# A mixture-of-experts layer on one core: the smallest of experts 2 to 31 is computed last, for 64 places instead of 96

## The reference, cut to what matters

```python
def moe_ffn(h, router_w, router_b, w_up, b_up, w_down, b_down):
    tok = h.reshape(-1, d)                                   # 512 tokens
    logits = (tok @ router_w + router_b).astype(jnp.float32) # 32 experts
    top_vals, top_idx = lax.top_k(logits, TOP_K)             # 4 experts for each token
    gate_w = jax.nn.softmax(top_vals, axis=-1)
    ...
    gu = lax.ragged_dot(x_sorted, w_up, group_sizes) + b_up[e_sorted]    # 1024 -> 2048
    g, u = gu[:, :D_EXPERT], gu[:, D_EXPERT:]
    g = jnp.minimum(g, SWIGLU_LIMIT)
    u = jnp.clip(u, -SWIGLU_LIMIT, SWIGLU_LIMIT)
    act = (u + 1.0) * (g * jax.nn.sigmoid(SWIGLU_ALPHA * g))
    out = lax.ragged_dot(act, w_down, group_sizes) + b_down[e_sorted]    # 1024 -> 1024
    out = out * gate_w.reshape(-1)[order][:, None].astype(out.dtype)
    y = jax.ops.segment_sum(out, token_of, num_segments=n_tok)
```

## Time and profile before

| | us |
|---|---|
| median of three runs | 1942.35 |
| the profiled execution, its own time | 1940.7 |
| its span, first to last instruction | 1938.9 |
| PE busy in it | 1831.4 (94%) |
| mean of the DMA traffic over the span | 263 GB/s, 510.85 MB |
| granted TensorE clock, mean | 0.997 |

### The profile page before, as it was taken

One profiled execution on the slowest core, in us unless ns is written; L12 is line 12 of the kernel. 1 busy time (PEld: TensorE's weight loads), 2 busy tenths in 40 slices (PEclk: granted clock), 3 DMA queues, 4 the chain that ended last, 5 costly groups with the idle time before them and its releaser, 6 DMA issues.

```text
span 1938.9 us, 34408 instructions
## 1 busy us (share of the span) xinstructions
PE 1831.4 (94%) x14020; PEld 1084.0 (56%) x14020; DVE 705.5 (36%) x1106; ACT 473.2 (24%) x729; POOL 102.8 (5%) x137
## 2 busy tenths in 40 slices
PE   6999999999999999989999988998899889989998
PEld 4777788888888888843343332433333333333346
DVE  5666768887765345361000000000000000000056
ACT  3444443525435243220110000101000000000036
POOL 2000001001020000000000000000000000000030
PEclk9999999999999999999999999999999999999999
DMA  4333322222222443279999999999999999999962
GB/s 131 88 87 102 94 76 66 66 65 65 65 66 66 118 143 109 112 316 408 400 421 425 422 425 423 424 423 423 424 422 422 421 424 416 420 422 421 387 228 105
DMA packets 171005, 510.85 MB, mean 263 GB/s; under 512 B 14293, under 2 KB 124838, under 8 KB 138118
## 3 DMA queue, kind: packets, MB, share of 16 engines
q1 hardware_dynamic: 154480, 474.67, 62.5%
q10 hardware_dynamic: 9494, 17.58, 2.7%
q0 software_dynamic: 6912, 16.79, 2.4%
HBM read 497.79 MB, written 19.60 MB: 267 GB/s over the span
## 4 chain that ended last, share of the span: by engine, by line
PE 77%; DMA 15%; DVE 4%; ACT 2%; issue 1%; ACTq 0%; DVEq 0%; POOL 0%; SPq 0%
PE psum L2026 73%; DMA arena<-in_w_up 15%; PE psum L2417 1%; PE psum L2426 1%; DVE arena L1445 1%; PE psum L2088 0%; PE psum L2196 0%; DMA arena<-y_dram,rows_u 0%; PE psum L2156 0%; ACT w_hi L817 0%; PE psum L2141 0%; DVE w_lo L1329 0%; DVE arena L1513 0%; DVE arena L1359 0%; DVE arena L1424 0%
## 5 line engine op out<-in xcount | busy, mean ns | idle before, releaser
L2026 PE MATMUL psum<-arena 128*32 128x512 f32 (+3 forms) x9344 | 981.9, 538 | 71.2 <-DMA arena<-in_w_up 58.9
L2026 PEld LDWEIGHTS psum<-arena 128*32 128x32 f32 (+2 forms) x9344 | 388.6, 116 | 613.7 <-issue 432.0
L1879 DVE TENSOR_SCALAR arena<-psum 128x768 f32<-128x768 f32 (+1 forms) x32 | 26.9, 841 | 906.9 <-ACT arena L1142 906.9
L2026 PE MATMUL psum<-h_hi,w_hi 128*128 128x512 f32 x640 | 258.7, 404 | 1.3 <-DVE w_lo L1329 1.3
L2026 PE MATMUL psum<-h_hi,w_lo 128*128 128x512 f32 x640 | 249.9, 390 | 0.0
L2026 PE MATMUL psum<-h_lo,w_hi 128*128 128x512 f32 x640 | 249.4, 390 | 0.0
L1329 DVE TENSOR_TENSOR w_lo<-arena,w_hi 128x1024 fp32r<-128x1024 f32 x104 | 135.6, 1305 | 187.7 <-ACT w_hi L817 186.7
L1142 ACT ACTIVATE arena<-psum 128x768 f32<-128x768 f32 (+1 forms) x32 | 22.9, 717 | 574.4 <-PE psum L2026 574.4
L2026 PEld LDWEIGHTS psum<-h_hi,w_hi 128*128 128x128 f32 x640 | 120.3, 188 | 33.9 <-issue 8.2
L2026 PEld LDWEIGHTS psum<-h_lo,w_hi 128*128 128x128 f32 x640 | 120.4, 188 | 26.4 <-issue 2.9
L2026 PEld LDWEIGHTS psum<-h_hi,w_lo 128*128 128x128 f32 x640 | 120.1, 188 | 25.9
(11 more groups left out here) (383 smaller groups left out, 1623.1 us busy)
## 6 DMA issues: line engine op xcount, KB each, us to landing
arena<-in_w_up SPq DMA_DIRECT2D x128, 2048.0 KB, 25.7
arena<-in_w_down SPq DMA_DIRECT2D x128, 1024.0 KB, 26.0
arena<-in_w_in SPq DMA_DIRECT2D x80, 512.0 KB, 3.9
arena<-in_w_ssd_branch SPq DMA_DIRECT2D x16, 512.0 KB, 4.0
y_dram<-arena ACTq DMA_DIRECT2D x17, 288.0 KB, 7.1
y_dram<-arena ACTq DMA_DIRECT2D x8, 512.0 KB, 4.0
arena<-in_w_attn_branch SPq DMA_DIRECT2D x8, 512.0 KB, 3.9
arena<-in_w_out SPq DMA_DIRECT2D x8, 512.0 KB, 4.4
```

The lines of the kernel that those rows point to most:

```text
L1879: dve.tensor_scalar(u_sb[:, 0:n], up_psum[:, 0:n, 1, :], 1.0 + LIMIT, 1.0 - LIMIT, ALU.min, ALU.max).then_inc(u_ready, 1)
L2026: return pe.matmul(o, l, r, start=start, stop=stop)
```

## The change

Block 31 becomes a small block, and its expert is no longer fixed. Experts 2 to 31 are all sorted. The one with the fewest tokens is block 31, the next 14 are the small blocks of the pairs, and all others are large, so 15 blocks have 64 places. `FLAG` now asks whether the 15th smallest has over 64 tokens, and `AGAIN` becomes 36. Since the expert of block 31 is known only late, its rows in `y_dram` are filled with zeros by two ACT DMAs of 128 KB each, after `swish(0)` (`clear_last`), from rows that a longer memset on DVE leaves at zero, and the early DMA of 256 KB is gone. The sort runs on all 128 partitions instead of one, since `hot_last` now needs the row number of the last expert on each of them (`last_row`).

```diff
-SMALLS, FIRST_SMALL, PAIR = 14, 3, 64
+SMALLS, FIRST_SMALL, PAIR = 15, 3, 64
+PAIRS = SMALLS - 1
...
-        last_hot = at(MOE_AT + 13, TT * TOPK, CAP)
-        last_slots = at(MOE_AT + 25, TT, CAP)
+        last_hot = at(MOE_AT + 13, TT * TOPK, PAIR)
+        last_slots = at(MOE_AT + 25, TT, PAIR)
...
+        no_rows = at(ARENA - 2, 512)[PAIR:P]
+        last_row = sb("last_row", [P, 1])
...
-            load_down(EXPERTS - 1, EXPERTS - 1)
-            load_bias_down(EXPERTS - 1, EXPERTS - 1)
+            e = owner_of(EXPERTS - 1)
+            load_down(EXPERTS - 1, e)
+            load_bias_down(EXPERTS - 1, e)
...
-            last_row = (EXPERTS - 1) * CAP
-            act.dma_start(y_dram[last_row:last_row + PAIR], zero_rows[0:PAIR]).then_inc(y_zeroed, 16)
...
+            def clear_last():
+                at_block = act.value_load(control[0:1, EXPERTS - 1:EXPERTS], min_val=0, max_val=EXPERTS - 1)
+                for half in range(2):
+                    act.dma_start(y_dram[ds(at_block * CAP, PAIR), half * 512:half * 512 + 512], no_rows).then_inc(y_zeroed, 16)
...
             swish(0)
+            clear_last()
             copy_last_slots()
...
-            swish(EXPERTS - 1)
+            swish(EXPERTS - 1, small=True)
...
-            copy_act(EXPERTS - 1)
+            copy_act(EXPERTS - 1, small=True)
...
-            dve.memset(arena[:, kb(MOE_AT + 28):kb(MOE_AT + 32)], 0.0)
+            dve.memset(arena[:, kb(MOE_AT + 28):kb(ARENA)], 0.0)
...
-            sorted_of = slice(2, EXPERTS - 1)
+            sorted_of = slice(2, EXPERTS)
...
-            key = [by_size[0:1, i, sorted_of] for i in range(3)]
+            key = [by_size[:, i, sorted_of] for i in range(3)]
...
+            dve.tensor_copy(control[:, EXPERTS - 1:EXPERTS], small_of[0:1, 0:1])
+            own.mark(dve.tensor_scalar(last_row[:], small_of[:, 0:1], float(CAP), None, ALU.mult))
...
-                own.then(dve.tensor_scalar(row_f, row_f, float((EXPERTS - 1) * CAP), None, ALU.subtract))
+                own.then(dve.tensor_scalar(row_f, row_f, last_row[:], None, ALU.subtract))
...
-            take_u(EXPERTS - 1)
-            join(EXPERTS - 1)
+            take_u(EXPERTS - 1, small=True)
+            join(EXPERTS - 1, small=True)
...
-                        if k < 2 * STRIPS:
-                            ins = mm(bank(half)[0:CAP], act_T[:, k, 0:CAP], w[:, cols], k == 0, False)
-                        else:
-                            for j in range(STRIPS):
-                                ins = mm(bank(half)[strip(j)], act_strip(k, j), w[:, cols], False, False)
+                        c = k // 2
+                        tokens = act_T[:, 2 * (c % 2) + k % 2, PAIR * (c // 2):PAIR * (c // 2 + 1)]
+                        ins = mm(bank(half)[0:PAIR], tokens, w[:, cols], k == 0, False)
...
-                up(EXPERTS - 1, range(STRIPS))
+                up_small(EXPERTS - 1)
                 down(EXPERTS - 2)
-                turn_act(EXPERTS - 1, last=True)
+                turn_act(EXPERTS - 1, last=True, small=True)
                 down_last(EXPERTS - 1)
```

More of the change, by code:

```diff
@@ L767, in _ @@
             extra = pool.value_load(control[0:1, FLAG:FLAG + 1], min_val=0, max_val=AGAIN)
-            pool.wait_ge(y_zeroed, 16 * (HEADS + 1))
+            pool.wait_ge(y_zeroed, 16 * (HEADS + 2))
             with pool.If(extra > 0):
@@ L771, in _ @@
                 pool.wait_ge(y_stored, 32 * (ROUNDS - 1))
+                pool.wait_ge(y_zeroed, 16 * (HEADS + 4))
                 gather_rows(BLOCKS * CAP)
@@ L1043, in _ @@
             root(GROUPS - 1)
-            act.wait_ge(y_zeroed, 16 * (HEADS + 1))
+            act.wait_ge(y_zeroed, 16 * HEADS)
             take_gate(GS0)
@@ L1841, in _ @@
             dve.tensor_copy(control[:, FLAG:FLAG + 1], owner[0:1, 31:32]).then_inc(tables_ready, 1)
-            own.mark(dve.max_index(small_at[0:1, 8:16], smallest[0:1, 8:16], key[1]))
-            own.then(dve.scalar_tensor_tensor(out=key[2], in0=key[0], scalar=smallest[0:1, SMALLS - 1:SMALLS],
-                                              in1=iota_far[0:1, sorted_of], op0=ALU.is_lt, op1=ALU.mult))
-            own.mark(dve.tensor_copy(small_of[0:1], small_at[0:1]))
-            own.then(dve.max(others[0:1, 0:8], key[2]))
@@ L1849, in _ @@
-            own.mark(dve.tensor_scalar(small_of[0:1], small_of[0:1], 2.0, None, ALU.add))
-            own.then(dve.scalar_tensor_tensor(out=key[1], in0=key[2], scalar=others[0:1, 7:8], in1=key[2],
+            own.mark(dve.max_index(small_at[:, 8:16], smallest[:, 8:16], key[1]))
+            own.then(dve.scalar_tensor_tensor(out=key[2], in0=key[0], scalar=smallest[:, SMALLS - 1:SMALLS],
+                                              in1=iota_far[:, sorted_of], op0=ALU.is_lt, op1=ALU.mult))
+            own.mark(dve.tensor_copy(small_of, small_at))
@@ L1851, in _ @@
+            own.then(dve.max(others[:, 0:8], key[2]))
+            own.mark(dve.tensor_scalar(small_of, small_of, 2.0, None, ALU.add))
+            own.then(dve.scalar_tensor_tensor(out=key[1], in0=key[2], scalar=others[:, 7:8], in1=key[2],
                                               op0=ALU.is_lt, op1=ALU.mult))
-            own.then(dve.max(others[0:1, 8:16], key[1]))
+            own.then(dve.max(others[:, 8:16], key[1]))
             own.then(dve.tensor_scalar(other_of[0:1], others[0:1], -1.0 / P, float(EXPERTS - 1), ALU.mult, ALU.add))
-            dve.tensor_copy(control[:, 2:4 + 2 * SMALLS].rearrange("o (q c) -> o q c", c=2)[:, :, 0],
-                            other_of[0:1, 0:SMALLS + 1])
@@ L2430, in strip, with up @@
                 return slice(STRIP * j, STRIP * (j + 1))
-            def up(b, order=STRIP_ORDER):
+            def up(b):
                 pe.wait_ge(x_copied, b + 1)
@@ L2440, in up @@
                         for j in range(STRIPS):
[L2441 removed]
+                            mm(bank(r)[strip(j)], x_T[:, k, strip(STRIP_ORDER[j])],
                                up_both[k][:, :, r * QUARTER:(r + 1) * QUARTER], k == 0, False)
[L2443 removed]
+                        ins = mm(bank(r)[strip(STRIPS)], x_T[:, k, strip(STRIP_ORDER[r])], up_both[k][:, :, WIDE:FF],
                                  k == 0, False)
@@ L2594, in sum_last @@
             def sum_last(t):
-                tokens = slots_last[0:CAP, t * P:(t + 1) * P]
+                tokens = slots_last[0:PAIR, t * P:(t + 1) * P]
                 for i, n in ((0, 0), (0, 1), (1, 0), (1, 1), (0, 2), (1, 2)):
```

43 lines of the change are left out of this document (23 added, 20 removed).

## The result

| | before | after |
|---|---|---|
| median of 13 runs each, us | 1942.93 | 1947.37 |
| their range | 1941.04 to 1946.38 | 1944.48 to 1948.97 |
| the profiled execution, its own time | 1940.7 | 1944.48 |
| its span | 1938.9 | 1942.4 |
| granted clock, mean over the span | 0.997 | 0.994 |

The ratio is 1.002, with a 95% interval from 1.0012 to 1.0027. The means lie 3.85 ± 1.24 us apart. The changed kernel is slower by 0.2%, just where the measurement begins to tell. The forecast was 1940.9 us, no change that can be told, with 1943.8 us as the range's upper end.

The account below looks back on a forecast made before the run. The weight stream was taken to set the pace, with PE binding only at the expert stage's end. The sum -2.1 - 0.44 + 0.62 + 0.46 = -1.5 us on a 1942.35 us median gave 1940.9 us, range 1937.6 to 1943.8.

Parts of the forecast that it names:

- the clock as a rival: After up_small(31)'s waits the clock falls to 1.2 GHz, costing down(30) or the last k 1.7 us: 1942.5 us, chance 0.10.
- The shorter end: End of the expert stage: small up(31) gains 2.1 us, turn_act(31) 0.23 and copy_act(31) 0.21.
- The landing: Last w_up chunk of up(31) still lands some 24 us after issue, at 1843.0, holding up_small(31)'s end to 1847.3 us.
- its sign of being wrong altogether: Last landings moving by more than 1.1 us against the start of the stage, in either direction.
- the first rival: Chunks of up(31) already there, so up_small(31) ends 6.6 us earlier: sum -6.0, 1936.4 us; chance 0.12.
- down_last at nothing: 16 matmuls of 64 places replace 12 of 96 and 12 strips: counted as nothing, could bring 0.2 us.
- the gathers bind: After down_last the third gather, landed at 1876.03 and added until 1877.4 us, binds, so a down_last gain would not show.
- The memset and the casts: DVE: longer memset in table building costs 0.46 us; one cast and one tensor_scalar delay up(0) by 0.2, nothing at the end.
- The zeros: 256 KB of stores moved into the full weight stream make every later landing 0.62 us late, bounds 0 and 1.2.

Follow-up runs that it names:

- d2: Kernel before, block 31 still large, with only sum_last contracting over the first 64 of its 96 rows: 1945.65 us, +3.30 ± 1.09 us against before.
- e2: Changed kernel with only the sum widened to 96 rows, down_last still 64 wide: 1943.82 us, +0.08 ± 0.94 us against the kernel before.
- b1: Kernel before with only the end of the change, block 31 small and its expert still 31: 1943.48 us, +0.14 ± 1.16 us against before.
- d1: Kernel before with block 31 small and expert 31, but down_last 96 wide and sum_last over 96 rows: 1939.93 us, -2.40 ± 1.50 us against before.
- b2: Kernel before with only the start: long memset, sort on 128 partitions, last_row, zeros in the stream; block 31 large: 1945.39 us, +1.92 ± 0.68 us.
- c2: Kernel before with down_last's last two k as single matmuls instead of strips: 1942.07 us, -0.86 ± 0.99 us against before.
- e4: Kernel before with only the zeros moved into the full stream and their memset behind hot_last: 1943.28 us, -0.24 ± 0.87 us against before.
- c4: Changed kernel with the short memset, zero rows set behind hot_last and stored after swish(31): 1943.48 us, +0.82 ± 1.09 us against the kernel before.
- d3: Changed kernel with the short memset and the zeros stored just after copy_act(0): 1946.32 us, +2.71 ± 1.72 us against the kernel before.
- d4: Changed kernel with late zeros, short memset, down_last 96 wide and sum_last over 96 rows: 1941.75 us, -0.37 ± 1.57 us against the kernel before.
- e3: Repeat of the changed kernel with late zeros, short memset, down_last and sum_last both 96 wide: 1942.16 us, -1.14 ± 1.62 us against the kernel before.
- c3: Changed kernel with the early 256 KB DMA of zeros kept beside the new ones: 1946.27 us, +3.08 ± 1.07 us against the kernel before.

## Why the prediction was wrong

**The step that failed** is one that isn't in the sum: the change part by part ends with down_last and prices nothing behind it. `sum_last` got 64 rows instead of 96, and the prediction doesn't name it: it stands at nothing without a reason. Its matmuls do last as long as before (0.61 us for the first two after, 0.62 before), and that is not the whole price. I did have the clock as a rival, but placed its fall after the waits of up_small(31), for 1.7 us and at a chance of 0.10. There it came in none of the thirteen profiles with a small block 31; in this one the last chunk took 3.64 us and down(30) 10.57 at full clock. It came 35 us after the last of these waits, at 1880.8 us, and cost 3.56 us in the pair of profiles and 1.2 to 3.8 us over the runs (d2: 3.30; e2 against the changed kernel: 0.08 against 3.20 and 3.85). The forecast's -1.5 and the measured +3.85 lie 5.3 us apart (its base, the median of three runs, was another 0.6 us under that of thirteen). The tails' average of 2.5 us explains about half of it; the rest stands under what stays open.

How 10.2 us at half clock make only 3.56 us: PE isn't the bound in all of it. From the bias of down_last to the first gate matmul it is 8.79 us before and 10.01 us after, so 1.22 us of the loss are here; another 1.10 went into PE's wait for DVE, which shrank from 1.47 to 0.37 us. The other 2.34 us are the gate projection: some 12 matmuls that start every 0.43 us instead of every 0.23 us.

**The shorter end was right.** up(31), turn_act and copy_act were to give 2.1 + 0.23 + 0.21 = 2.54 us by the start of down_last. b1 shows 2.56, but so close a match of one pair is luck: from up(0) to down_last the profiles take 1002.2 to 1004.2 us with a large block 31 (five) and 998.9 to 1002.9 with a small one (thirteen), 1003.1 and 1000.9 on average, since the stream comes in earlier or later by up to some 4 us. d1's own profile, at 1002.85, shows no gain at all. A measure free of this drift starts at PE's last wait in block 29, that for its fourth chunk. (The profile of the kernel before has no such wait, since the clock fell just ahead of it.) In b1, and in b2 with its large block 31:
```profile
1780.71 3.64 PE L2027 MATMUL psum<-arena 128*32 128x512 f32 x32 [1.47 <-DMA arena<-in_w_up]
...
1784.88 3.64 PE L2034 MATMUL psum<-arena 128*32 128x512 f32 x32 [1.26 <-DMA arena<-in_w_up]
...
1865.91 14.10 PE L2034 MATMUL psum<-arena 128*96 128x512 f32 x48 [0.90 <-ACT arena L1168]
```
From there to down_last it is 81.03 us in b2 (and within 0.01 us of it in c2, d2 and e4), 78.79 in b1 and 78.6 to 78.9 in the ten others with a small block 31 that have this wait. So the gain is 2.1 to 2.5 us in every one of these executions, for the forecast's 2.54.

The landing, the number on which the sum rested, held in this pair: the last chunk of w_up in the profile after was issued at 1821.4 us, and its row says
```profile
L559 SPq DMA_DIRECT2D arena<-in_w_up x1: 333/333/333, 1821.4 to 1821.4; - x1
...
DMA to landing us min/median/max: 24.3/24.3/24.3
```
24.3 us against 24.1 in the earlier trace rows, and 1821.4 + 24.3 = 1845.7 is where PE's wait ends, 983.1 us after the start of up(0) against 983.3 before. In the other profiles with a small block 31 this is 982.5 to 986.5 us, which passes the 1.1 us that the prediction named as its sign of being wrong altogether. It wasn't, since the same drift moves the kernels with a large block 31. The Trainium skill ("DMA: Bandwidth & Descriptors", "Latency and other measured facts") says that DMA engines 7 and 15 are usually slower; the trace agrees in that the landing time stayed, and shows of no engine which it is. The whole gain, the first rival, is out with it. down(30) had no wait, as forecast.

**down_last at nothing** was right to 0.15 us (13.88 to its bias against 14.03). That even a gain there wouldn't show, since the gathers bind, was tested by no run.

**The memset and the casts.** DVE after, as in the earlier trace rows:
```profile
837.73 1.34 DVE L1765 MEMSET arena<- 128x1536 f32 x1 [0.26 <-issue]
...
857.55 0.13 DVE L1869 CAST control<-arena 1x1 int32<-1x1 f32 x1
857.62 0.13 DVE L1870 TENSOR_SCALAR last_row<-arena 128x1 f32<-128x1 f32 x1
```
From the same router matmuls as in the balance to up(0) it is 29.5 to 29.7 us in the kernels with neither, 29.7 to 29.9 with the casts and the short memset (c4, d3, d4, e3) and 30.2 to 30.4 with both: 0.2 us for the casts and 0.5 for the memset, just what the forecast had (0.2 and 0.46).

**The zeros** were put at 0.62 us, and none was found (e4: -0.24 ± 0.87, so 0.62 isn't excluded). ACT's two issues come just after up(0), and its next copy starts when PE's four transposes are done; copy_act(0) at 890.20 us still waited 2.13 us for PE:
```profile
886.20 1.24 ACTq L1188 DMA_DIRECT2D y_dram<-arena  x2
887.49 0.59 ACT L1175 ACTIVATE slots_last<-psum 64x512 fp32r<-64x512 f32 x1 [1.18 <-PE psum L2561]
```

**What stays open.** By its parts the start half should cost 0.7 to 0.8 us, and b2 shows 1.92 ± 0.68. c4 is 2.1 to 2.4 us under its neighbours, for the memset's 0.5 us and zeros whose cost was not found. And d4 should have d1's gain less 0.2 us, and shows -0.37 and -1.14 for -2.40; the intervals overlap. So there may be another microsecond or more in the start half, or the intervals, of ± 0.7 to ± 1.7 us, mislead by so much. No run here tells these apart. Nor is it known why fewer rows bring the clock down. In the timed runs the link of clock and time within one kernel is weak (-0.24 ± 0.13 us for each 0.001 of mean clock, over the 191 runs of the changed kernel and the experiments), and the stream's drift, of the same size, may hide it. The link stands on the comparison of kernels and on the tails of the profiles.

## What to carry to other kernels

When a change makes the last block smaller, follow the new size past the block, into every matmul that reads its output, and ask of each not only how long it takes but what it does to the clock of the dense work behind it. A matmul with fewer rows may cost the same time and still be the more expensive one. Keep the contraction at its old width: zeros in the spare rows cost nothing that could be told here (e2: +0.08 ± 0.94), and in d1 the gain of the shorter block then showed (-2.40). In the whole change it didn't. And let the range include the clock wherever short matmuls with waits stand ahead of a dense stretch, since one profile without a fall doesn't say that the next has none.

## What the runs showed of the hardware

- The rows that a matmul contracts over bear on TensorE's clock. The same sequence with the same lengths kept 2.4 GHz more often with 96 rows than with 64 (2.3 against 9.5 us at 1.2 GHz in the tail, nine profiles each; 12 of 224 against 58 of 102 runs with a low clock; 3.30 ± 1.09 us of time in d2). In the profile after there is no idle time ahead of the fall beyond the 1.2 us for ACT and the short gaps in `sum_last`, and PE was busy for 1.83 of the 2 us from 1878 us on and all the time from there to the fall. The Trainium skill ("TensorE: Matmul & The Clock Gate", "HAM oscillation — how this bites in real kernels") tells of falls that come from long idle gaps in a matmul loop that waits for DMA. The falls here are not of that kind: PE's last wait for DMA ends over 30 us ahead of them.
- The waits for w_up between the chunks of up_small(31), 0.7 to 1.8 us long, brought no fall of the clock in any of the thirteen profiles with a small block 31. The like waits of block 29, of 0.3 to 2.0 us, have a fall beside them in four of the eighteen (before, c3, c4, e3).
- 256 KB of stores added to a stream that runs at 416 to 425 GB/s through most of 980 us could not be seen in the time (-0.24 ± 0.87 us, which leaves room for the 0.6 us of their bytes).
- The same kernel's weight stream brings its last chunk 2 us earlier or later from one execution to the next (983.1 us after the start of up(0) in one profile of the changed kernel, 985.2 in the other; 982.5 to 986.5 over the thirteen profiles with a small block 31).
